# First weights and tokens in parts, the dense block's last h ahead of the next weights, the last expert h turned inside a down product

## The chip, the cores and the metric

One core of a Trainium2 chip runs the whole kernel. The metric is the device time of one execution in microseconds (us); a lower time is better.

## The reference, cut to what matters

Two layers over 256 tokens of width 1024, all float32. Each layer has a mixer and a feed-forward part, each followed by a LayerNorm of the scaled residual.

```python
for i in range(2):
    mix = hybrid_mixer(x, ...)           # proj = x @ w_in (1024 x 2560), split in b, c, h, u, v
    x = layer_norm(ALPHA * x + mix, ...) # gated short convolution | spatial gating of gelu(v); @ w_out
    if i % 2 == 0: ffn = (silu(x @ wg) * (x @ wu)) @ wd                  # dense, width 2816
    else:          ffn = sum over 8 experts, two chosen for each token   # width 3584 each
    x = layer_norm(ALPHA * x + ffn, ...)
```

## The kernel before, in words

**Tiling.** The 256 tokens are two tiles of 128. Weights come as 397 pieces of 1 MB (128 partitions x 2048 elements), numbered in the order of use. SyncE (SP) loads piece p into slot p % 6 of `raw` (`load`, L255) and waits, from piece 6 on, until piece p - 6 has been split. ScalarE (ACT) rounds a piece to `w_hi` (`split_hi`, L395), VectorE (DVE) writes the rest to `w_lo` (`split_lo`, L633), and TensorE (PE) makes each product as three matmuls: high by high, low by high, high by low (`product`, L1017). `w_hi` and `w_lo` have four places, so piece p waits until piece p - 4 has been used. The activations are split in the same way: `t_hi`/`t_lo` hold the turned tokens (xT), `a_hi`/`a_lo` the mixer output, the dense h or the gathered tokens of an expert, and `hT_hi`/`hT_lo` the turned h of an expert step.

**Order.** Every engine has its own list, written by hand; nothing is planned at run time.

**Start.** SP issues both token tiles (one DMA each), pieces 0 and 1 (the v columns of `w_in`), the two rows `v_g` and `v_b`, pieces 2 and 3, `w_s`, pieces 4 and 5, `b_s`, and so on (L267 to L292). PE turns both token tiles (`transpose_x(0, n)`, L1103), ACT and DVE split the turned tokens and then pieces 0 to 3 (L419, L721), and PE makes v for tile 0 and then tile 1, from piece 0 and then piece 1 (`tile_columns`, L1036; 24 matmuls of 256 columns for each of the four blocks). Then come two pieces with 48 such matmuls each (`two_blocks`, L1051), and then the transposes of `chan_rows` and `ws_raw`, for which GpSimd (POOL) must have masked `w_s` (L345).

**End of the dense block.** Groups of 256 hidden columns, j = 0 to 10. In group 10, ACT rounds piece 47 (the first of layer 1), waits for the gate and up products, takes the silu (L486), rounds piece 48 (L487) and then rounds h (L494). DVE multiplies (L826), splits piece 48 (L827) and then writes the rest of h (L830). PE ends with `last_rows` (L1085): for token tile 0 the down products of groups 9 and 10, then the same for tile 1. Before the last half of tile 1 it turns token tile 0, which DVE's `layer_norm` (L667) must have normalised.

**End of the experts.** 56 steps (8 experts x 7). In step i PE makes the gate product, turns the h of step i - 1 (`transpose_h`, L1242), makes the up product and then `down(i - 1)` (L1282), in two halves of 12 matmuls of 512 columns. After step 55 nothing is left but to turn its h, wait for ACT (L523) and DVE (L892) and make `down(55)`. Then the result is split, scattered to the tokens, added and normalised.

**Placement.** Tensors lie in SBUF in the order of their declaration (L82 to L122). `hT_hi`, `hT_lo`, `ys_hi`, `ys_lo`, `pickT` and the mixer's `work`, `v_rows`, `bs_rows` and `wsT` stand behind `chan`, `wr`, `small`, `eps_rms`, `neg_half` and `most_i`.

## Time and profile before

| | us |
|---|---|
| median of 3 runs | 1420.73 |
| lowest, highest | 1418.74, 1420.90 |
| the profiled execution | 1418.72 |
| its span in the trace | 1417.0 |
| PE busy | 1382.3 (98%) |
| DVE busy | 1120.4 (79%) |
| ACT busy | 905.2 (64%) |

The page of the profile has the busy time of each engine, the span in 40 slices, the DMA queues, the chain of work that ended last and the costliest groups of instructions. L12 is line 12 of the kernel. A wait is put down to what came last; idle time of an engine counts only where the end hangs on it. The granted clock is the share of PE's full clock (2.4 GHz); 0.50 is 1.2 GHz. The end of a matmul is modelled, so its pace is better read from the starts of matmuls that follow each other.

### The profile page before, as it was taken

Reading aid. Unit: us, or ns where it says so; the run is one execution under the profiler, and the core shown is the slowest. Engines: PE = TensorE matmul, PEld = TensorE weight load, DVE = VectorE, ACT = ScalarE, POOL = GpSimd, SP = SyncE. Lnnn points to the kernel's source line nnn. Section 1 sums busy time; section 2 is a strip of 40 time slices with the busy share of each in tenths; the row PEclk is TensorE's granted clock in tenths of the full one; section 3 lists DMA queues with packets and bytes.
Section 4 is the critical chain, followed back from the end, with each engine's and each line's share of the span. In section 5 each row is a group of like instructions: output and inputs, shape, how many; then the busy total and the mean of one; then the engine's idle time right before and its main releaser. Section 6 shows DMA issues by size and latency. Waiting matters only on the chain.

```text
span 1417.0 us, 17126 instructions
## 1 busy us (share of the span) xinstructions
PE 1382.3 (98%) x7250; PEld 1176.6 (83%) x7250; DVE 1120.4 (79%) x799; ACT 905.2 (64%) x657; POOL 21.5 (2%) x37
## 2 busy tenths in 40 slices
PE   7999999999999999999999999999999999999995
PEld 7979999989778888888888888888888888888883
DVE  6676454477779889879888988888898899889885
ACT  5374333444767777777677777777777676777771
POOL 1000000010000000000000000000000000000001
PEclk9999999999999999999999999999999999999998
DMA  9846655546459999999999999999999999999980
GB/s 324 307 143 220 194 181 180 191 137 215 141 176 391 367 353 365 348 338 365 360 349 348 357 361 337 363 364 344 348 359 354 349 364 364 342 353 353 365 321 31
DMA packets 202420, 425.89 MB, mean 301 GB/s; under 512 B 7740, under 2 KB 51812, under 8 KB 202340
## 3 DMA queue, kind: packets, MB, share of 16 engines
q1 hardware_dynamic: 201248, 421.06, 83.7%
q0 software_dynamic: 1024, 3.67, 0.8%
q8 instruction: 59, 0.97, 0.3%
q14 instruction: 21, 0.17, 0.0%
q10 hardware_dynamic: 68, 0.02, 0.0%
HBM read 423.68 MB, written 1.05 MB: 300 GB/s over the span
## 4 chain that ended last, share of the span: by engine, by line
PE 75%; DVE 2%; ACT 1%; issue 0%; DVEq 0%; ACTq 0%
PE turn L1020 15%; PE turn L1022 15%; PE turn L1021 15%; PE accp L1020 8%; PE accp L1022 8%; PE accp L1021 8%; PE accp L1245 2%; PE accp L1232 2%; PE accp L1272 1%; DVE w_lo L631 1%; ACT w_hi L400 0%; PE accp L1043 0%; PE accp L1048 0%; PE accp L1044 0%; PE turn L1272 0%; PE turn L1232 0%
## 5 line engine op out<-in xcount | busy, mean ns | idle before, releaser
L631 DVE TENSOR_TENSOR w_lo<-raw,w_hi 128x2048 fp32r<-128x2048 f32 x397 | 908.4, 2292 | 211.3 <-ACT w_hi L400 207.7
L400 ACT CAST w_hi<-raw 128x2048 fp32r<-128x2048 f32 x397 | 759.1, 1914 | 259.0 <-PE turn L1022 151.6
L1020 PE MATMUL turn<-w_hi,a_hi 128*128 128x512 f32 x888 | 352.8, 397 | 0.4 <-DVE w_lo L631 0.4
L1022 PE MATMUL turn<-w_hi,a_lo 128*128 128x512 f32 x888 | 347.4, 391 | 0.0
L1021 PE MATMUL turn<-w_lo,a_hi 128*128 128x512 f32 x888 | 346.1, 390 | 0.0
L1022 PEld LDWEIGHTS turn<-w_hi,a_lo 128*128 128x128 f32 x888 | 166.7, 188 | 36.6
L1021 PEld LDWEIGHTS turn<-w_lo,a_hi 128*128 128x128 f32 x888 | 167.0, 188 | 33.7
L1020 PEld LDWEIGHTS turn<-w_hi,a_hi 128*128 128x128 f32 x888 | 166.8, 188 | 33.7 <-DVE w_lo L631 0.8
L1020 PE MATMUL accp<-w_hi,hT_hi 128*128 128x512 f32 x448 | 178.5, 398 | 1.4 <-DVE hT_lo L631 1.4
L1022 PE MATMUL accp<-w_hi,hT_lo 128*128 128x512 f32 x448 | 176.9, 395 | 0.0
L1021 PE MATMUL accp<-w_lo,hT_hi 128*128 128x512 f32 x448 | 176.8, 395 | 0.0
L1020 PE MATMUL turn<-t_hi,w_hi 128*128 128x256 f32 x576 | 163.3, 283 | 0.0
L1022 PE MATMUL turn<-t_hi,w_lo 128*128 128x256 f32 x576 | 163.0, 283 | 0.0
L1021 PE MATMUL turn<-t_lo,w_hi 128*128 128x256 f32 x576 | 163.0, 283 | 0.0
L1021 PEld LDWEIGHTS turn<-t_lo,w_hi 128*128 128x128 f32 x576 | 110.5, 192 | 0.4
L1020 PEld LDWEIGHTS turn<-t_hi,w_hi 128*128 128x128 f32 x576 | 110.5, 192 | 0.3
L1022 PEld LDWEIGHTS turn<-t_hi,w_lo 128*128 128x128 f32 x576 | 110.5, 192 | 0.0
L1020 PEld LDWEIGHTS accp<-w_hi,hT_hi 128*128 128x128 f32 x448 | 84.4, 188 | 20.3 <-DVE hT_lo L631 1.6
L1022 PEld LDWEIGHTS accp<-w_hi,hT_lo 128*128 128x128 f32 x448 | 84.3, 188 | 20.0
L1021 PEld LDWEIGHTS accp<-w_lo,hT_hi 128*128 128x128 f32 x448 | 84.5, 189 | 18.8
L1020 PE MATMUL accp<-w_hi,a_hi 128*128 128x512 f32 x152 | 61.5, 405 | 3.5 <-DVE a_lo L631 3.5
L519 ACT ACTIVATE y_work<-turn 128x512 f32<-128x512 f32 x56 | 33.6, 599 | 46.0 <-PE turn L1022 40.6
(175 smaller groups left out, 958.1 us busy)
## 6 DMA issues: line engine op xcount, KB each, us to landing
raw<-in_we_gate SPq DMA_DIRECT2D x112, 1024.0 KB, 6.9
raw<-in_we_up SPq DMA_DIRECT2D x112, 1024.0 KB, 7.1
raw<-in_we_down SPq DMA_DIRECT2D x112, 1024.0 KB, 6.8
raw<-in_w_in SPq DMA_DIRECT2D x20, 1024.0 KB, 6.6
raw<-in_w_gate SPq DMA_DIRECT2D x11, 1024.0 KB, 5.3
raw<-in_w_up SPq DMA_DIRECT2D x11, 1024.0 KB, 5.3
raw<-in_w_down SPq DMA_DIRECT2D x11, 1024.0 KB, 5.0
raw<-in_w_out SPq DMA_DIRECT2D x8, 1024.0 KB, 7.6
```

The lines of the kernel that those rows point to most:

```text
L400: nc.scalar.copy(w_hi[:, p % PARTS, :], raw[:, p % RING, :]).then_inc(hi_done, 1)
L519: nc.scalar.activation(silu_e[:, i % 2, :], turn[:, 2 * (i % 2), :], ACT.Silu).then_inc(e_silu, 1)
L631: return nc.vector.tensor_tensor(out, whole, hi.bitcast(f32), ALU.subtract)
L1020: nc.tensor.matmul(to, lh, rh, start=start, stop=False, **group)
L1021: nc.tensor.matmul(to, lh, rl, start=False, stop=False, **group)
L1022: return nc.tensor.matmul(to, ll, rh, start=False, stop=stop, **group)
L1232: last = nc.tensor.matmul(to[:, k - k0, :], part[:, n, k * P:(k + 1) * P], pick[:, n, :], start=(n == 0), stop=(n == NT - 1))
L1245: last = nc.tensor.transpose(accp[:, 2, b * P:(b + 1) * P], h[:, b * P:(b + 1) * P], ident[:])
L1272: last = nc.tensor.matmul(to, pickT[:, n * P:(n + 1) * P], part[:, cols], start=(i == 0), stop=(i == 1))
```

## The change

- **Placement.** `chan` is made 64 elements wide in place of 40, `eps_rms` and `neg_half` move into unused columns of `small`, and `most_i` is made 16 elements wide. Tensors take whole steps of 32 bytes, so `wr`, `slot_iota`, `rank` and `small` move up by 96 bytes, and everything declared behind `most_i` by 96 - 64 + 32 = 64 bytes.
- **Start.** SP issues the columns of token tile 0 in two DMAs, piece 0 in four, token tile 1 in two and piece 1 in two. `v_g`, `v_b` move behind pieces 2 and 3, `w_s` behind pieces 4 and 5, `b_s` behind 6 and 7. PE makes six products of `ident` with itself ahead of the turning of tile 0 and four behind it. ACT and DVE split piece 0 in four parts and piece 1 in two. PE makes the v blocks in the order piece 0 tile 0, piece 0 tile 1, piece 1 tile 0, piece 1 tile 1, part by part, and turns tile 1 ahead of the last part of piece 0's first block. `split_done` and `hi_done` count from piece 2 on.
- **Gelu of tile 0.** ACT waits for the last matmul of tile 0's v instead of the next block's, in both layers.
- **End of the dense block.** In group 10 ACT takes the silu once the gate piece is used, and rounds h ahead of piece 48; DVE waits for the up piece ahead of the multiplication, and writes the rest of h ahead of piece 48.
- **End of the experts.** PE turns the h of step 55 between the halves of `down(54)`. ACT and DVE split it in halves of 256 columns, the second when `down(54)` has ended, and the second half of `down(55)` waits for it.

The diff, cut to its core (`first_hi` and `first_lo` of before are also renamed to `slots_hi` and `slots_lo`):

```diff
+    FIRST = ((0, 0, 2), (0, 2, 4), (0, 4, 6), (0, 6, 8), (1, 0, 4), (1, 4, 8))
     def dense_gate(j):
...
-        chan = sb("chan", [P, N_CHAN])
+        chan = sb("chan", [P, 64])
         wr = sb("wr", [P, KD, E])
...
         small = sb("small", [P, 208])
-        eps_rms = sb("eps_rms", [P, 1])
-        neg_half = sb("neg_half", [P, 1])
-        most_i = sb("most_i", [1, 1], i32)
+        most_i = sb("most_i", [1, 16], i32)
         with ExitStack() as mixers:
...
         rstd = small[:, 20:24]
+        eps_rms = small[:, 24:25]
+        neg_half = small[:, 25:26]
         logits = small[:, 32:48].rearrange("p (n e) -> p n e", n=NT)
...
-        x_loaded = [sem(f"x_loaded{n}") for n in range(NT)]
+        x_loaded = [[sem(f"x_loaded{n}{half}") for half in range(2)] for n in range(NT)]
+        first_filled = [sem(f"first_filled{c}") for c in range(len(FIRST))]
+        first_hi, first_split, v0_done = sem("first_hi"), sem("first_split"), sem("v0_done")
         ws_loaded, chan_loaded, vrows_loaded, bs_loaded, ln_loaded, wr_loaded = (
...
             return p + 1
+        def split_of(p):
+            return (first_split, (4, 6)[p]) if p < 2 else (split_done, p - 1)
+        def fills(p):
+            return p // RING + (1 if p % RING > 1 else 0)
         def transposed(build, n, half=1):
...
                 if p >= RING:
-                    sp.wait_ge(split_done, upto(p - RING))
+                    sp.wait_ge(*split_of(p - RING))
                 dst = raw[:, p % RING, :].rearrange("p (k f) -> p k f", k=src.shape[1])
...
                     for half in range(2):
-                        load(at + 2 * i + half, columns(w_in[l], c0 + half * HALF))
+                        if l or i:
+                            load(at + 2 * i + half, columns(w_in[l], c0 + half * HALF))
                     between(i)
...
             def small_inputs(i):
+                if i == 2:
+                    sp.dma_start(ws_raw, w_s.rearrange("l h t s -> t (l h) s")).then_inc(ws_loaded, 16)
                 if i == 1:
-                    sp.dma_start(ws_raw, w_s.rearrange("l h t s -> t (l h) s")).then_inc(ws_loaded, 16)
-                if i == 0:
                     for j, a in enumerate((v_g, v_b)):
                         sp.dma_start(v_rows[:, j, :], a[0].partition_broadcast(P)).then_inc(vrows_loaded, 16)
-                if i == 2:
+                if i == 3:
                     sp.dma_start(bs_rows[:], b_s.partition_broadcast(P)).then_inc(bs_loaded, 16)
...
                     sp.dma_start(wr[:], w_router[0].rearrange("(k p) e -> p k e", p=P)).then_inc(wr_loaded, 16)
-            for n in range(NT):
-                sp.dma_start(x[:, n, :], x_in[0, n * P:(n + 1) * P, :]).then_inc(x_loaded[n], 16)
+            def load_x(n):
+                for half in range(2):
+                    cols = slice(half * BANK, (half + 1) * BANK)
+                    sp.dma_start(x[:, n, cols], x_in[0, n * P:(n + 1) * P, cols]).then_inc(x_loaded[n][half], 16)
+            def load_first(p):
+                src = columns(w_in[0], 3 * CW + GW + p * HALF)
+                dst = raw[:, p, :].rearrange("p (k f) -> p k f", k=KD)
+                for c, (piece, k0, k1) in enumerate(FIRST):
+                    if piece == p:
+                        sp.dma_start(dst[:, k0:k1, :], src[:, k0:k1, :]).then_inc(first_filled[c], 16)
+            load_x(0)
+            load_first(0)
+            load_x(1)
+            load_first(1)
             mixer(0, 0, small_inputs)
...
-                act.wait_ge(slot_filled[p % RING], 16 * (p // RING + 1))
+                act.wait_ge(slot_filled[p % RING], 16 * fills(p))
                 if p >= PARTS:
...
+            def first_parts(p):
+                for c, (piece, k0, k1) in enumerate(FIRST):
+                    if piece == p:
+                        act.wait_ge(first_filled[c], 16)
+                        part = slice(k0 * HALF, k1 * HALF)
+                        nc.scalar.copy(w_hi[:, p, part], raw[:, p, part]).then_inc(first_hi, 1)
             for n in range(NT):
                 round_tile(0, n)
-            splits(0, 3)
+                first_parts(n)
+            splits(2, 3)
             for l in range(DEPTH):
...
                 for n in range(NT):
-                    used(at + n)
+                    if n:
+                        used(at + 1)
+                    else:
+                        act.wait_ge(v0_done, l + 1)
                     nc.scalar.activation(v[:, n, :], accp[:, n, :], ACT.Gelu).then_inc(v_gelu, 1)
...
                             split_hi(p)
-                        used(dense_up(j))
+                        used(dense_up(j) if j < GROUPS - 1 else dense_gate(j))
                         gate = accp[:, 0:2, 0:HALF] if j == 0 else turn_half[:, 4 * (j % 2):4 * (j % 2) + 2, :]
                         nc.scalar.activation(silu_buf[:, j % 2], gate, ACT.Silu).then_inc(silu_ready, 1)
-                        split_hi(p + 1)
+                        if j < GROUPS - 1:
+                            split_hi(p + 1)
                         if j == 0:
...
                             nc.scalar.copy(h_hi[:, j % 2], h_buf[:, j % 2]).then_inc(h_hi_ready, 1)
-                        if j < GROUPS - 1:
-                            split_hi(p + 2)
+                        split_hi(p + 2 if j < GROUPS - 1 else p + 1)
                     round_tile(2, 0)
...
+            def round_last_h():
+                act.wait_ge(e_hT, N_STEPS)
+                for half in range(2):
+                    if half:
+                        used(step_down(N_STEPS - 2) + 1)
+                        act.wait_ge(e_hT_lo, N_STEPS)
+                    cols = slice(half * HALF, (half + 1) * HALF)
+                    nc.scalar.copy(hT_hi[:, cols], accp[:, 2, cols]).then_inc(e_hT_hi, 1)
             def round_ys(e):
...
             split_hi(MOE_AT + MOE_PIECES - 1)
-            round_h(N_STEPS - 1)
+            round_last_h()
             round_ys(E - 1)
...
-                dve.wait_ge(hi_done, upto(p))
+                dve.wait_ge(hi_done, p - 1)
                 rest_of(w_lo[:, p % PARTS, :], raw[:, p % RING, :], w_hi[:, p % PARTS, :]).then_inc(split_done, 1)
...
             last.then_inc(mean_conv_ready, 1)
-            for n in range(NT):
-                rest_of_tile(0, n)
-            splits(0, 3)
+            def first_part(c):
+                p, k0, k1 = FIRST[c]
+                dve.wait_ge(first_hi, c + 1)
+                part = slice(k0 * HALF, k1 * HALF)
+                rest_of(w_lo[:, p, part], raw[:, p, part], w_hi[:, p, part]).then_inc(first_split, 1)
+            for half in range(2):
+                rest_of_xT(0, 0, half, turn[:, half, :].rearrange("p (k t) -> p k t", t=P))
+                first_part(half)
+            first_part(2)
+            first_part(3)
+            rest_of_tile(0, 1)
+            first_part(4)
+            first_part(5)
+            splits(2, 3)
             for l in range(DEPTH):
...
                         dve.wait_ge(silu_ready, j + 1)
+                        used(dense_up(j))
                         nc.vector.tensor_tensor(h_buf[:, j % 2], up, silu_buf[:, j % 2], ALU.mult).then_inc(h_whole, 1)
-                        split_lo(p + 1)
+                        if j < GROUPS - 1:
+                            split_lo(p + 1)
                         dve.wait_ge(h_hi_ready, j + 1)
...
                         rest_of(h_lo[:, j % 2], whole, h_hi[:, j % 2]).then_inc(h_ready, 1)
-                        if j < GROUPS - 1:
-                            split_lo(p + 2)
+                        split_lo(p + 2 if j < GROUPS - 1 else p + 1)
                     layer_norm(1, MIX1_AT - 1)
...
                 rest_of(hT_lo[:], accp[:, 2, :], hT_hi[:]).then_inc(e_hT_lo, 1)
+            def rest_of_last_h():
+                for half in range(2):
+                    dve.wait_ge(e_hT_hi, N_STEPS + half)
+                    cols = slice(half * HALF, (half + 1) * HALF)
+                    rest_of(hT_lo[:, cols], accp[:, 2, cols], hT_hi[:, cols]).then_inc(e_hT_lo, 1)
             def rest_of_ys(e):
...
             split_lo(MOE_AT + MOE_PIECES - 1)
-            rest_of_h(N_STEPS - 1)
+            rest_of_last_h()
             def finish_experts():
...
-                if build == 0:
-                    pe.wait_ge(x_loaded[n], 16)
                 for half in range(2):
-                    if build:
+                    if build == 0:
+                        pe.wait_ge(x_loaded[n][half], 16)
+                    else:
                         pe.wait_ge(ln_norm, transposed(build - 1, n, half))
...
                         pe.wait_ge(xT_ready, transposed(build, n, 2 * k // KD))
+                    last = nc.tensor.matmul(to, xT_lo[:, k, tile], wh[:, k, :], start=False, stop=(k == KD - 1))
+                return last
+            def first_columns(p, n, to, before_last=None):
+                tile = slice(n * P, (n + 1) * P)
+                wh, wl = [a[:, p, :].rearrange("p (k f) -> p k f", k=KD) for a in (w_hi, w_lo)]
+                for c, (piece, k0, k1) in enumerate(FIRST):
+                    if piece != p:
+                        continue
+                    if k1 == KD and before_last is not None:
+                        before_last()
+                    pe.wait_ge(first_hi, c + 1)
+                    for k in range(k0, k1):
+                        if k in (0, KD // 2):
+                            pe.wait_ge(xT_hi_ready, transposed(0, n, 2 * k // KD))
+                        nc.tensor.matmul(to, xT_hi[:, k, tile], wh[:, k, :], start=(k == 0), stop=False)
+                    pe.wait_ge(first_split, c + 1)
+                    for k in range(k0, k1):
+                        nc.tensor.matmul(to, xT_hi[:, k, tile], wl[:, k, :], start=False, stop=False)
+                for k in range(KD):
+                    if k in (0, KD // 2):
+                        pe.wait_ge(xT_ready, transposed(0, n, 2 * k // KD))
                     last = nc.tensor.matmul(to, xT_lo[:, k, tile], wh[:, k, :], start=False, stop=(k == KD - 1))
...
                             last.then_inc(piece_used, 1)
+            def warm(count):
+                for _ in range(count):
+                    nc.tensor.matmul(turn[:, 3, 0:P], ident[:], ident[:], start=True, stop=True)
             pe.wait_ge(ident_ready, 1)
-            for n in range(NT):
-                transpose_x(0, n)
+            warm(6)
+            transpose_x(0, 0)
+            warm(4)
+            for half in range(2):
+                for n in range(NT):
+                    last = first_columns(half, n, accp[:, n, half * HALF:(half + 1) * HALF],
+                                         (lambda: transpose_x(0, 1)) if half == 0 and n == 0 else None)
+                    if n:
+                        last.then_inc(piece_used, 1)
+                    elif half:
+                        last.then_inc(v0_done, 1)
             for l in range(DEPTH):
                 at = l * MIX1_AT
-                for n in range(NT):
-                    if l and n:
+                for n in range(NT if l else 0):
+                    if n:
                         transpose_x(2, 1)
                     for half in range(2):
-                        last = tile_columns(at + half, 2 * l, n, accp[:, n, half * HALF:(half + 1) * HALF])
+                        last = tile_columns(at + half, 2, n, accp[:, n, half * HALF:(half + 1) * HALF])
                         if n:
                             last.then_inc(piece_used, 1)
+                        elif half:
+                            last.then_inc(v0_done, 1)
                 for i in range(2):
...
                 for half in range(2):
+                    if half and i == N_STEPS - 2:
+                        pe.wait_ge(e_h, N_STEPS)
+                        transpose_h(h_e[:, (N_STEPS - 1) % 2, :]).then_inc(e_hT, 1)
+                    if half and i == N_STEPS - 1:
+                        pe.wait_ge(e_hT_lo, N_STEPS + 1)
                     half_down(half, split(step_down(i) + half), s == 0 and half == 0,
...
-                if i:
+                if 0 < i < N_STEPS:
                     pe.wait_ge(e_h, i)
```

## Rows read from the trace of the kernel before

**Rows 1.** The page: its span, and the busy time of each engine.
```profile
span 1417.0 us, 17126 instructions
...
PE 1382.3 (98%) x7250; PEld 1176.6 (83%) x7250; DVE 1120.4 (79%) x799; ACT 905.2 (64%) x657; POOL 21.5 (2%) x37
```

**Rows 2.** PE's waits: waiting line, awaited line, us in all, times, longest.
```profile
PE accp L1043 <- DVE w_lo L631: 5.2, 1, 5.2
...
PE accp L1020 <- DVE a_lo L631: 3.5, 3, 2.7
...
PE accp L1020 <- DVE hT_lo L631: 1.4, 1, 1.4
```

**Rows 3.** Timeline of the start: start, us, engine, line, operation, idle before and releaser.
```profile
1.24 0.29 POOL L329 TENSOR_SCALAR_AFFINE_SELECT ident<-ident 128x128 f32<-128x128 f32 x1 [0.24 <-POOL ident L327]
...
4.57 3.36 PE L1033 MATMUL turn<-ident,x 128*128 128x128 f32 x16 [4.57 <-DMA x<-in_x]
...
8.85 1.90 ACT L400 CAST w_hi<-raw 128x2048 fp32r<-128x2048 f32 x1 [0.30 <-DMA raw<-in_w_in]
...
13.13 0.58 PE L1043 MATMUL accp<-w_hi,t_hi 128*128 128x256 f32 x1 [5.20 <-DVE w_lo L631]
...
17.23 1.91 ACT L400 CAST w_hi<-raw 128x2048 fp32r<-128x2048 f32 x1 [3.52 <-DMA raw<-in_w_in]
...
18.12 0.28 PE L1043 MATMUL accp<-w_hi,t_hi 128*128 128x256 f32 x1
...
22.09 1.09 POOL L345 TENSOR_SCALAR_AFFINE_SELECT y_work<-y_work 128x1024 f32<-128x1024 f32 x1 [19.28 <-DMA y_work<-in_w_s]
...
26.75 0.28 PE L1020 MATMUL turn<-t_hi,w_hi 128*128 128x256 f32 x1
```

**Rows 4.** Windows of the start: busy us (count) by engine, granted clock, DMA share, GB/s.
```profile
5.00:10.00 5.00, 2.92 (x16) 2.69 (x14) 2.67 (x4) 3.47 (x5) 0.00 (x0) 1.00 1.08 358
10.00:15.00 5.00, 1.87 (x8) 1.88 (x9) 3.55 (x2) 2.65 (x2) 0.00 (x0) 0.59 1.06 307
```

**Rows 5.** Timeline of the end of the dense block.
```profile
281.92 0.60 ACT L486 ACTIVATE y_work<-turn 128x512 f32<-128x512 f32 x1 [3.81 <-PE turn L1022]
...
282.55 0.69 DVE L826 TENSOR_TENSOR y_work<-turn,y_work 128x512 f32<-128x512 f32 x1 [2.11 <-ACT y_work L486]
...
284.21 0.62 ACT L494 CAST a_hi<-y_work 128x512 fp32r<-128x512 f32 x1
...
284.24 0.39 PE L1022 MATMUL accp<-w_hi,a_lo 128*128 128x512 f32 x1
...
287.30 0.74 PE L1020 MATMUL accp<-w_hi,a_hi 128*128 128x512 f32 x1 [2.67 <-DVE a_lo L631]
...
290.28 0.69 DVE L677 SCALAR_TENSOR_TENSOR x<-x,accp 128x512 f32<-128x512 f32 x1 [3.03 <-issue]
...
295.15 1.42 DVE L692 SCALAR_TENSOR_TENSOR x<-x,small,ln_rows 128x512 f32<-128x512 f32 x2
...
295.96 1.32 PE L1033 MATMUL turn<-ident,x 128*128 128x128 f32 x8
```

**Rows 6.** A window behind that wait, with the columns of rows 4.
```profile
288.00:289.00 1.00, 1.00 (x4) 0.81 (x3) 0.00 (x0) 0.00 (x0) 0.00 (x0) 0.50 0.89 250
```

**Rows 7.** Timeline of the end of the experts.
```profile
1386.46 2.28 DVE L631 TENSOR_TENSOR w_lo<-raw,w_hi 128x2048 fp32r<-128x2048 f32 x1
...
1389.77 0.60 PE L1245 MATMUL accp<-ident,y_work 128*128 128x128 f32 x4
...
1391.77 0.51 PE L1020 MATMUL accp<-w_hi,hT_hi 128*128 128x512 f32 x1 [1.40 <-DVE hT_lo L631]
```

**Rows 8.** The page's groups: count, busy us, mean ns of one, idle before.
```profile
L631 DVE TENSOR_TENSOR w_lo<-raw,w_hi 128x2048 fp32r<-128x2048 f32 x397 | 908.4, 2292 | 211.3 <-ACT w_hi L400 207.7
...
L1021 PE MATMUL turn<-w_lo,a_hi 128*128 128x512 f32 x888 | 346.1, 390 | 0.0
...
L1021 PE MATMUL accp<-w_lo,hT_hi 128*128 128x512 f32 x448 | 176.8, 395 | 0.0
```

32 lines of the change are left out of this document (16 added, 16 removed).

## Prediction

> **What bounds the kernel now.** I read the page first: PE is busy for 1382.3 of 1417.0 us, so only what lets PE work without a gap, or work less, can move the end [rows 1]. Then I read PE's own waits, to see where the other 35 us are [rows 2]: one wait of 5.2 us for the split of piece 0, behind a start in which PE has nothing but two token tiles; one of 2.7 us (the longest of three on that line) for the last dense h; one of 1.4 us for the last expert h. The change has one part for each. The timelines around these three places give the durations [rows 3, 5, 7], the windows give the clock and the rate of the transfers [rows 4, 6], and the page's groups show what else the change touches [rows 8]. Between the three places PE is the engine that others wait for, so what is won at one place shifts all that follows (the transfers behind the first six pieces wait for freed slots, L257).
>
> **The start, PE's side.** Before, the v blocks begin at 13.13 and the fourth ends at 26.75. The first block's 24 matmuls take 4.99 us (0.208 each), the next 72 take 8.63 us (0.120 each) [rows 3]: PE came out of a pause of 5.2 us, the granted clock is 0.59 on average between 10 and 15 us [rows 4], and the pace says it went from 1.2 to 2.4 GHz just ahead of 18.12.
>
> **The start, transfers.** Two tiles and piece 0 are 2.10 MB and have landed at 8.85 [rows 3]; the rate is 358 GB/s [rows 4]. So a transfer that ends after c MB lands at 8.85 - (2.10 - c) / 0.358. In the new order: tile 0 at 3.7 and 4.4, the quarters of piece 0 at 5.2, 5.9, 6.6 and 7.4, tile 1 at 8.85, the halves of piece 1 at 10.3 and 11.8, piece 2 at 14.7 (it was 17.23 [rows 3]), piece 3 at 17.6.
>
> **The start, the chain.** `ident` is ready at 1.53. A transpose took 0.21 us (3.36 / 16) [rows 3]; the trace has no product of `ident` with itself, so each costs 0.21 as the transpose does, or 0.42 if a product in full float32 takes two such passes. I take 0.42: the six end at 4.1, with no loss against tile 0 at 3.7 to 4.4 beyond 0.4 us. Tile 0 is turned by 5.8. ACT takes 0.62 us for 512 columns [rows 5]: the two halves of tile 0 end at 5.8 and 6.65, the quarters of piece 0 at 7.3, 7.9, 8.5 and 9.15, each behind its landing. DVE takes 0.69 us for 512 [rows 5], in its order: rest of quarter 0 until 8.05, second half of tile 0 until 8.75, quarters 1, 2 and 3 until 9.45, 10.15 and 10.85. So PE, which follows the quarters, is limited by DVE. It ends quarter 2 at 10.45, turns tile 1 (8 x 0.12) until 11.4, makes quarter 3 (4 x 0.12) and the eight matmuls with the tokens' low part by 12.9. Three more blocks of 24 x 0.12 = 2.88 end at 21.5. Before it was 26.75: **5.2 us** earlier. The four products behind tile 0 run from 5.8 to 7.5 at most, while PE has nothing to do until 7.3, so they cost nothing.
>
> **The start, what is late next.** Piece 1: ACT needs 1.05 us for 1024 columns (between 0.62 for 512 and 1.90 for 2048), DVE 1.22 in the same way from 0.69 and 2.29 [rows 3, 5, 8]; behind tile 1 that gives 14.5 and 15.7 for its halves, and PE asks at 15.8 and 16.8. Piece 2 lands at 14.7, is split at 18.9 and wanted at 21.5. The moved small tensors: `v_g` and `v_b` land with piece 3, near 20, ahead of the first gelu. `w_s` was there at 22.09 with 6.29 MB issued, 1.5 us later than the line above gives; now 8.39 MB precede its end, so 28 to 29.5, the mask takes 1.1 [rows 3], and PE asks at 21.5 + 96 x 0.12 = 33.0. Cover of 2.4 us; if it is gone, each further microsecond costs one. SP issues ten DMAs for four, ahead of data that moves for 9 us; nothing waits for SP there.
>
> **The clock in the start.** Both ends: if the low clock lasted until 17.7 as it did before, quarter 3 and tile 1 would end at 14.7 instead of 12.9, some 14 matmuls more would run at 0.208, and the fourth block would end at 24.6: a gain of 2.1. If the products cost 0.21 and the clock is up early, the chain moves by 0.8: a gain of 6.0. I take 5.2, because PE is now busy from 1.6 to 7.5 almost without a gap, longer than the 4.6 us of work after which the clock rose before, and no idle stretch behind it is over 1.4 us. The Trainium skill, TensorE: Matmul & The Clock Gate (What's actually happening), says that the low clock is the default and activity lifts it; by that rule the added products do what the rows lead me to take.
>
> **The end of the dense block.** PE's 12 matmuls of tile 0 with group 9 start at 281.72 (284.24 - 11 x 0.229) and the next could start at 284.47; it started at 287.30 [rows 5], and the microsecond after 288 shows 4 matmuls at granted clock 0.50 [rows 6], 0.43 each against 0.23, for about 3.4 us: 2.8 us of waiting and 1.6 us of low clock. Now DVE multiplies from 281.95 to 282.65, ACT rounds h until 283.3 (0.62), DVE ends the rest at 284.05 (0.69): 0.4 us ahead of PE's need, so both are gone for PE. But piece 48 now comes behind: ACT until 285.2, DVE until 287.5 (2.29 [rows 8]), and only then can the LayerNorm begin, which could have begun at 286.1. It began at 290.28 and reached its last step at 295.15, and PE turned the tile at 295.96 [rows 5]. With its start at 287.5 and 0.2 us of waiting gone, PE turns it at 293.0: **2.9 us** earlier. PE has work only until 284.47 + 30 x 0.229 = 291.3, so a new wait of 1.7 us stands there. Bounds: 4.4 if the LayerNorm were no limit, 1.2 if the new wait costs the clock again (1.7 us, half of 3.4). The added wait of DVE for the up piece holds nothing in groups 0 to 9, where the silu waited for it already.
>
> **The end of the experts.** `down(54)` starts at 1384.2 (24 x 0.232 ahead of 1389.77) and its half at 1387.0; the h of step 55 is ready at 1386.5, just ahead of DVE's piece at 1386.46 to 1388.74 [rows 7]. The four transposes cost 0.48 there (4 x 0.12), as they did behind. ACT and DVE have the first half of h at 1389.2, and `down(55)` starts at 1384.2 + 24 x 0.232 + 0.48 = 1390.25 instead of 1391.77; the second half of h comes near 1391.2 and is wanted at 1393.0. **1.5 us** earlier; bounds 1.0 and 1.6. The gelu of tile 0 in layer 1 may start earlier; no wait of PE hangs on it: nothing.
>
> **The realigned tensors.** Not one row of ACT or DVE hangs on them. What moves and matters is `hT_hi` and `hT_lo`: their 1344 matmuls take 395 ns each where those with `a_hi` and `a_lo` take 390 [rows 8]. That difference may come from where they lie; a move by 64 bytes may then take it away (-6.7 us, 1344 x 0.005), leave it, or raise it by as much. I take nothing: the rows do not show which address is good. The Trainium skill, SBUF — State Buffer (Two separate sides, the note on cachelines), knows lines of 16 bytes only; both places begin on one, so by it nothing changes either.
>
> **Sum.** 5.2 + 2.9 + 1.5 = 9.6 us. The profiled execution took 1418.72, its span 1417.0, with 1.7 us around it; it gives 1409.1. The median is 2.0 us above that execution, so the median comes to **1411.1 us**.
>
> **Rivals.**
> (a) The clock stays low through the first blocks, because PE works in short bursts between 7.5 and 12.9: the start gives 2.1. 1414.2 us. For it: the 0.50 behind a gap of 2.7 us [rows 5, 6]; against it: the gaps here are half as long. 12%.
> (b) The new wait of 1.7 us at the dense end brings the low clock back: 1412.8 us. 8%.
> (c) The change doesn't do what it says at the start, since transfers in small parts are slower or land in no order: at 307 GB/s in place of 358 [rows 4], the 3.15 MB up to piece 1 and the 2.10 up to tile 1 come 1.0 to 1.5 us later, and PE, held by tile 1 at 10.45, loses up to as much with each of them, and piece 2 loses its cover: a gain of 1 to 3 in place of 5.2. 1414.5 us. The Trainium skill, SBUF — State Buffer (The DMA setup-cost knee), speaks against this part of the change: it wants the largest single transfer; by its 224 GB/s for 256 KB, an estimate of mine puts tile 1 at 12.3 in place of 8.85, some 2 us too late for PE. 8%.
> (d) The move of `hT` takes the 5 ns away: 1404.4 us. 8%.
> (e) Slower than before: the move of `hT` makes each of its 1344 matmuls slower. From 7.1 ns on (9.6 / 1344) it eats the whole gain; at twice the difference of the rows, 10 ns, it gives 1424.5 us. 4%; below 7 ns, near 1418, another 2%.
>
> The forecast itself has 58%.
>
> **How the numbers follow.** The forecast holds 1409 to 1412.5 by its terms; (a), (b) and (c) lie up to 1416. The range 1407.5 to 1416.5 takes these in, with 1.5 us for the scatter of the median, and leaves (d) and (e) out: 14% and the tails. 0.2% of 1420.73 is 2.8 us, about what a measurement of this kernel can tell from no change. Faster than that, below 1417.9: 94%; within it: 3%; slower: 3%.
>
> **What would show it.** In the changed kernel the first `two_blocks` matmul starts near 21.5 and its clock is 1.00 from about 9 us on; a start near 24.5 with 0.50 before is (a); PE waiting for a DMA is (c). No wait for the dense h, the transposes of the next tile near 288 (293.0 less 5.2), a wait of 1.7 us for the normalised x ahead of them, clock 1.00. No wait for `hT_lo` at the end. The mean of `accp<-w_lo,hT_hi` at 395 ns; 390 is (d), over 400 is (e). A `w_s` mask later than 33 us would make the prediction wrong at a place where I see cover.

## The result, and the profile after

The changed kernel takes **1406.3 us** (median of 13 executions, 1403.84 to 1416.54; before on the same chips 1420.73, 1418.19 to 1421.84). The ratio is 0.9904, 95% interval 0.9889 to 0.9918: faster, by 14.4 us where 9.6 were forecast. The sign, and the 2 us between a median and its profiled execution, came out as written; the time lies 1.2 us below the low end of the range of 1407.5 to 1416.5. One of the 13 executions took 1416.54 at a granted clock of 0.986; nothing here explains it.

The page of the changed kernel answers [rows 1]: the profiled execution took 1404.18, its span is 14.8 us shorter, and PE's busy time is 5.6 us shorter although 20 records were added. Work itself has become quicker, not only waits.

```profile
span 1402.2 us, 17198 instructions
PE 1376.7 (98%) x7270; PEld 1176.3 (84%) x7270; DVE 1119.4 (80%) x804; ACT 905.6 (65%) x662; POOL 21.4 (2%) x37
```

PE's waits in the changed kernel (waiting line, awaited line, us in all, times, longest), against [rows 2]. The waits of 5.2, 2.7 and 1.4 us are gone; what stands in their place is the wait for the normalised `x`, whose longest was 1.3 and is 1.5.

```profile
PE turn L1104 <- DVE x L742: 3.3, 4, 1.5
...
PE turn L1091 <- DVE w_lo L681: 1.1, 2, 0.7
PE accp L1091 <- DVE a_lo L681: 0.8, 2, 0.4
```

The timeline of the start (start, us, engine, line, operation, idle before and releaser), against [rows 3]:

```profile
1.58 2.93 PE L1199 MATMUL turn<-ident 128*128 128x128 f32 x12 [1.58 <-POOL ident L357]
...
4.30 1.91 PE L1104 MATMUL turn<-ident,x 128*128 128x128 f32 x8
...
6.01 1.12 PE L1199 MATMUL turn<-ident 128*128 128x128 f32 x8
...
7.41 0.51 PE L1135 MATMUL accp<-w_hi,t_hi 128*128 128x256 f32 x2 [0.28 <-ACT w_hi L453]
...
10.28 1.03 PE L1104 MATMUL turn<-ident,x 128*128 128x128 f32 x8
...
13.41 1.05 ACT L453 CAST w_hi<-raw 128x1024 fp32r<-128x1024 f32 x1 [0.43 <-DMA raw<-in_w_in]
...
14.49 1.23 DVE L681 TENSOR_TENSOR w_lo<-raw,w_hi 128x1024 fp32r<-128x1024 f32 x1 [0.25 <-ACT w_hi L453]
...
16.42 1.91 ACT L428 CAST w_hi<-raw 128x2048 fp32r<-128x2048 f32 x1 [1.96 <-DMA raw<-in_w_in]
...
16.91 0.64 PE L1138 MATMUL accp<-w_lo,t_hi 128*128 128x256 f32 x4
...
21.23 0.28 PE L1091 MATMUL turn<-t_hi,w_hi 128*128 128x256 f32 x1
```

The end of the dense block, against [rows 5]: h is split ahead of piece 48, PE never waits for it, and the LayerNorm (L727) starts right behind DVE's piece.

```profile
278.33 0.62 ACT L535 CAST a_hi<-y_work 128x512 fp32r<-128x512 f32 x1 [4.10 <-DVE y_work L890]
...
278.99 0.69 DVE L681 TENSOR_TENSOR a_lo<-y_work,a_hi 128x512 fp32r<-128x512 f32 x1 [0.69 <-ACT a_hi L535]
280.80 2.29 DVE L681 TENSOR_TENSOR w_lo<-raw,w_hi 128x2048 fp32r<-128x2048 f32 x1 [1.12 <-ACT w_hi L428]
283.00 0.68 DVE L727 SCALAR_TENSOR_TENSOR x<-x,accp 128x512 f32<-128x512 f32 x1
...
287.70 1.41 DVE L742 SCALAR_TENSOR_TENSOR x<-x,small,ln_rows 128x512 f32<-128x512 f32 x2 [0.22 <-DVE x L735]
288.51 1.32 PE L1104 MATMUL turn<-ident,x 128*128 128x128 f32 x8 [1.46 <-DVE x L742]
```

Two windows around that wait, with the columns of [rows 4]: the granted clock (third figure from the end) stays at 1.00, where [rows 6] has 0.50.

```profile
284.00:286.00 2.00, 2.00 (x11) 1.65 (x10) 1.90 (x4) 0.00 (x0) 0.00 (x0) 1.00 0.78 259
286.00:288.00 2.00, 1.05 (x5) 0.55 (x3) 1.77 (x4) 0.00 (x0) 1.00 (x1) 1.00 0.76 266
```

The end of the experts, against [rows 7]: the last h is turned 12 matmuls earlier, and no wait stands between it and the last product.

```profile
1374.05 0.60 PE L1355 MATMUL accp<-ident,y_work 128*128 128x128 f32 x4
...
1375.79 0.42 DVE L681 TENSOR_TENSOR hT_lo<-accp,hT_hi 128x256 fp32r<-128x256 f32 x1
...
1377.86 0.42 DVE L681 TENSOR_TENSOR hT_lo<-accp,hT_hi 128x256 fp32r<-128x256 f32 x1 [1.65 <-ACT hT_hi L573]
```

And the page's groups, against [rows 8]. The products with `a_hi` stand still at 390 ns; those with `hT_hi` went from 395 to 392.

```profile
L1092 PE MATMUL turn<-w_lo,a_hi 128*128 128x512 f32 x888 | 346.0, 390 | 0.0
...
L1092 PE MATMUL accp<-w_lo,hT_hi 128*128 128x512 f32 x448 | 175.7, 392 | 0.0
```

**Where the 14.75 us of the span went.** I cut both spans at the same seven matmuls, read from the timelines. For before these are the first of `two_blocks` at 26.75 [rows 3] (26.76 unrounded), the turning of token tile 0 at 101.49 (end of layer 0's mixer) and at 295.96 (end of the dense block, [rows 5]), that of tile 1 in the router stage at 391.74, and the first and last product with `hT`; three of the rows, of before:

```profile
101.49 1.21 PE L1033 MATMUL turn<-ident,x 128*128 128x128 f32 x7 [0.29 <-DVE x L692]
...
426.99 0.40 PE L1020 MATMUL accp<-w_hi,hT_hi 128*128 128x512 f32 x1
...
1397.22 0.40 PE L1022 MATMUL accp<-w_hi,hT_lo 128*128 128x512 f32 x1
```

and of the changed kernel:

```profile
97.07 0.66 PE L1104 MATMUL turn<-ident,x 128*128 128x128 f32 x4 [0.27 <-DVE x L742]
...
419.51 0.39 PE L1091 MATMUL accp<-w_hi,hT_hi 128*128 128x512 f32 x1
...
1382.52 0.39 PE L1093 MATMUL accp<-w_hi,hT_lo 128*128 128x512 f32 x1
```

| stretch | before | changed | difference | forecast |
|---|---|---|---|---|
| start, to the first `two_blocks` | 26.76 | 21.23 | -5.53 | -5.2 |
| mixer of layer 0 | 74.73 | 75.84 | **+1.11** | 0 |
| dense block, to the turned tile | 194.47 | 191.44 | -3.03 | -2.9 |
| mixer of layer 1, to the tile of the router stage | 95.78 | 95.75 | -0.03 | 0 |
| router stage, to the first product with `hT` | 35.25 | 35.25 | 0.00 | 0 |
| experts, first to last product with `hT` | 970.23 | 963.01 | **-7.22** | -1.5 |
| what follows | 19.76 | 19.71 | -0.05 | 0 |

The fourth stretch ends at 391.74 and 384.26. The start and the dense block are met within 0.4 us. Two stretches are not: the mixer of layer 0 gives back 1.1, and the experts gain 5.7 more than was forecast for the last h.

### The profile page after: what moved, and what is told of

Its sections match the earlier page's. It is cut to its first block, busy times and chain, and to the rows that moved or that the text cites. A ratio compares the mean times of both kernels' runs of the same rounds, so it can differ in the third digit from the quotient of the medians.

```text
span 1402.2 us, 17198 instructions
## 1 busy us (share of the span) xinstructions
PE 1376.7 (98%) x7270; PEld 1176.3 (84%) x7270; DVE 1119.4 (80%) x804; ACT 905.6 (65%) x662; POOL 21.4 (2%) x37
## 4 chain that ended last, share of the span: by engine, by line
PE 90%; DVE 4%; ACT 3%; SPq 1%; DMA 1%; issue 1%; POOL 0%; DVEq 0%; ACTq 0%
PE turn L1091 19%; PE turn L1093 19%; PE turn L1092 19%; PE accp L1091 9%; PE accp L1092 9%; PE accp L1093 9%; PE accp L1355 2%; PE accp L1342 2%; DVE w_lo L681 1%; PE accp L1382 1%; DMA y_work<-in_w_s 1%; ACT w_hi L428 1%; PE accp L1114 1%; SPq L272 1%; PE accp L1119 1%
## 5 line engine op out<-in xcount | busy, mean ns | idle before, releaser
L681 DVE TENSOR_TENSOR w_lo<-raw,w_hi 128x2048 fp32r<-128x2048 f32 (+1 forms) x401 | 907.9, 2269 | 204.3 <-ACT w_hi L428 200.1
L1091 PEld LDWEIGHTS accp<-w_hi,hT_hi 128*128 128x128 f32 x448 | 84.2, 188 | 17.7
```

What stands on the lines that cost most here:

```text
L681: return nc.vector.tensor_tensor(out, whole, hi.bitcast(f32), ALU.subtract)
L1091: nc.tensor.matmul(to, lh, rh, start=start, stop=False, **group)
```

## The experiments

Times of kernels are compared with before on the same chip. One execution of each kernel has a trace. Over these 14 traces three stretches repeat within 0.06 us where nothing in them was changed, and tell more than the medians: the dense block in its new order (191.41 to 191.45), the mixer of layer 1 (95.74 to 95.80) and the experts (within 0.02). The others differ between executions: the start with all ten products of `ident` takes 20.62 to 21.37 us, the mixer of layer 0 with the changed kernel's order 75.02 to 76.16, the router stage 35.2 to 38.7, and what follows the experts 18.7 to 19.8.

**1. Before, with `hT` moved by 64 bytes.** Is it the address of `hT` that makes the experts quicker? The edit, on the kernel before:

```diff
+        hT_pad = sb("hT_pad", [P, 16])
         hT_hi = sb("hT_hi", [P, COL], f32r)
```

> The kernel before with one edit: 64 unused bytes are declared ahead of hT_hi, so that hT_hi, hT_lo, ys_hi, ys_lo and pickT alone lie 64 bytes higher; chan, small, most_i and the mixer's tensors stay. Theory P (the place of hT sets the pace of the down products): the down products, 24 matmuls, go from 5.36 to 5.27 us (starts of first to last), accp<-w_lo,hT_hi from 395 to 392 ns, and the time falls by 56 x 0.096 = 5.4 us, to 1415.3. Rival Q (the pace fell because the small tensors or the work tensors moved, or because of the order of the work): 1420.7, 395 ns stays.

Measured: 1412.17 us against 1418.73, ratio 0.9956 (0.9941 to 0.9970). The experts' stretch takes 964.67 instead of 970.23, 5.57 us less. One padding tensor does well over a third of what the whole change does (5.57 of 14.75). It also moves `ys_hi`, `ys_lo` and `pickT`, and no run moves these alone; but 4.6 of the 5.57 us lie between the starts of neighbouring products with `hT`, so these are the main part. Another 0.97 us of the profiled execution lies in what follows the experts, which differs by as much between executions without this edit.

**2. The changed kernel with the small tensors placed as before.** The other side of the same question:

```diff
-        chan = sb("chan", [P, 64])
+        chan = sb("chan", [P, N_CHAN])
...
-        most_i = sb("most_i", [1, 16], i32)
+        eps_rms = sb("eps_rms", [P, 1])[:, :]
+        neg_half = sb("neg_half", [P, 1])[:, :]
+        most_i = sb("most_i", [1, 1], i32)
```

> The changed kernel with the placement of before (chan of 40 columns, eps_rms, neg_half and most_i as tensors of their own): everything else of the change stays. Theory P and rival Q with small tensors as the cause: 1406.3 + 5.4 = 1411.7 us, accp<-w_lo,hT_hi back at 395 ns. Rival Q with the order as the cause: 1406.3 us, 392 ns. The sum of my forecast without the placement was 1411.1.

Measured: 1412.05, ratio 0.9949 (0.9932 to 0.9965). The stretch takes 968.56; with the new placement it takes 963.01, 5.55 us less. The same amount from both kernels, and 968.56 against before's 970.23 leaves 1.67 us for the last h.

**3 and 4. `hT` moved further.** The changed kernel with 64 and with 192 bytes ahead of `hT_hi` (the same edit as in 1). In the compiled kernels `w_hi`, `w_lo` and the `a` and `t` tensors start at an address whose remainder by 256 is 128. For `hT_hi` it is 0 before, 64 in the changed kernel, 128 in the first of these runs and 0 again in the second.

> The changed kernel with 64 more unused bytes ahead of hT_hi, which puts hT at 128 bytes above a multiple of 512, as w_hi, w_lo, a_hi and a_lo lie. Theory P1 (the stationary operand is read without loss only where it lies as a_hi does): the steady pace goes from 229 to the 227 ns of the products with a_hi, 1344 x 0.0023 = 3 us less, 1403.2. Theory P2 (64 bytes off the old place is what counts): slower again than 1406.3, towards 1411.7. Rival Q: 1406.3.

> The changed kernel with 192 more unused bytes ahead of hT_hi: 256 above a multiple of 512. Theory P1: the pace of before or between, 229 to 233 ns, 1406 to 1411.7 us. If only the remainder by 256 counts, this is the place of before: 233 ns and 1411.7. Rival Q: 1406.3.

Measured: 1402.44, ratio 0.9879 (0.9863 to 0.9896), with the stretch at 960.10; and 1411.79, ratio 0.9947 (0.9930 to 0.9963), with the stretch at 968.56. So the pattern repeats after 256 bytes: the address 256 higher gives the stretch of the old place (run 2).

**5 and 6. Which rule?** Best at remainder 128: because that is a good place by itself, because it is the middle, or because the weights lie there too? In the first run `hT` is at 192 (128 bytes ahead of it). In the second the weights, the tokens and `hT` all move by 128 bytes against run 3, so all have remainder 0:

```diff
+        front_pad = sb("front_pad", [P, 32])
         raw = sb("raw", [P, RING, PIECE])
...
+        hT_pad = sb("hT_pad", [P, 16])
         hT_hi = sb("hT_hi", [P, COL], f32r)
```

> The changed kernel with 128 more unused bytes ahead of hT_hi: 192 above a multiple of 256, where before has 0, the change 64 and the best run so far 128. The 24 matmuls of a down product took 5.36, 5.27 and 5.21 us there. Theory M (what counts is the distance from 128, the remainder at which the weights w_hi and w_lo lie): 5.27 us and the time of the change, 1406.3. Rival N (the further up within 256 bytes the better): 5.21 us or less, 1403.

> 128 unused bytes ahead of raw and 64 ahead of hT_hi: every large tensor (raw, w_hi, w_lo, t, a) and hT now lie on a multiple of 256. Theory R (the stationary operand is best where its remainder by 256 equals that of the moving operand): all products at the best pace, 227 ns, time as with hT at 128: about 1403. Rival A (the place of the stationary operand alone counts, 0 is bad): the down products at 233 ns as before (+8.7 us against 1403) and the 2688 matmuls with a_hi and a_lo in the expert steps too, up to 6.5 ns each: another 17 us, about 1429.

Measured: 1409.94, ratio 0.9934 (0.9915 to 0.9953), stretch 968.28; and 1401.93, ratio 0.9870 (0.9854 to 0.9887), stretch 960.11. The second settles it: remainder 0 is as good as 128 if the weights have it too, and as bad as it was before if they haven't. What counts is how `hT` stands to the tensors ahead of it. All of these moved together, so the run doesn't single out one; the products with `hT` read only `w_hi` and `w_lo` of them, and I take it to be these. The page's group of these products, of before, of run 1, of run 3, of run 5 and of run 6, one fence each:

```profile
L1021 PE MATMUL accp<-w_lo,hT_hi 128*128 128x512 f32 x448 | 176.8, 395 | 0.0
```
```profile
L1022 PE MATMUL accp<-w_lo,hT_hi 128*128 128x512 f32 x448 | 175.7, 392 | 0.0
```
```profile
L1093 PE MATMUL accp<-w_lo,hT_hi 128*128 128x512 f32 x448 | 174.3, 389 | 0.0
```
```profile
L1093 PE MATMUL accp<-w_lo,hT_hi 128*128 128x512 f32 x448 | 177.1, 395 | 0.0
```
```profile
L1094 PE MATMUL accp<-w_lo,hT_hi 128*128 128x512 f32 x448 | 174.3, 389 | 0.0
```

| `hT` less weights, by 256 | runs | experts' stretch | against the best, per product |
|---|---|---|---|
| 0 | 3, 6, 11, 12 | 960.09 to 960.11 | 0 |
| -64 | changed, 7, 8, 9 | 963.01 | 2.2 ns |
| -128 | 2, 4 | 968.56 | 6.3 ns |
| +64 | 5 | 968.28 | 6.1 ns |

The last column is the difference divided by 1344. A matmul with 512 columns of the weights and 128 x 128 of `hT` as the operand that is loaded starts every 227 ns at best, as most of those with `a_hi` and `a_lo` do in all these kernels; at +64 the distances between starts alternate between 231 and 236 ns, and at -128 they run through a longer pattern from 228 to 241 ns.

**7. GpSimd's mask of `w_s` behind the first rstd.** What costs the mixer of layer 0 1.1 us? In the changed kernel GpSimd waits for `w_s` at the head of its list, and the power for v of token tile 0 (L378) is queued behind it; DVE (L797) waits for that power, and the split of the next piece is queued behind DVE's. The rows of the changed kernel:

```profile
28.92 1.09 POOL L373 TENSOR_SCALAR_AFFINE_SELECT y_work<-y_work 128x1024 f32<-128x1024 f32 x1 [26.11 <-DMA y_work<-in_w_s]
...
29.98 0.57 POOL L378 TENSOR_TENSOR small<-small 128x1 f32<-128x1 f32 x1
30.59 0.55 DVE L797 TENSOR_SCALAR work<-work,small 128x512 f32<-128x512 f32 x1 [5.95 <-POOL small L378]
...
34.85 0.39 PE L1091 MATMUL turn<-t_hi,w_hi 128*128 128x256 f32 x1 [0.74 <-DVE w_lo L681]
```

```diff
-            pool.wait_ge(ws_loaded, 16)
-            nc.gpsimd.affine_select(out=ws_raw, ...).then_inc(ws_masked, 1)
...
                 for n in range(NT):
                     power(v_var, v_rstd, n, NT * l + n + 1)
+                    if l == 0 and n == 0:
+                        pool.wait_ge(ws_loaded, 16)
+                        nc.gpsimd.affine_select(out=ws_raw, ...).then_inc(ws_masked, 1)
```

> The changed kernel with one move: GpSimd waits for w_s and masks it behind the power of v's tile 0 instead of ahead of it. Theory: in the changed kernel that power stood behind the wait for w_s (until 28.9 us), DVE waited 5.95 us for it, piece 4 was split late and PE waited 0.7 us; of the 5.5 us won by the first four blocks 1.1 was gone at the end of the mixer. So the turning of the tile behind the mixer comes at 96.0 in place of 97.07 and the time is 1405.2. Rival (the transfers behind it are late themselves): nothing, 1406.3.

Measured: 1404.46, ratio 0.9898 (0.9881 to 0.9914). In its timeline DVE's wait is 0.70 instead of 5.95, and PE has no wait between 26 and 41 us:

```profile
25.46 0.58 POOL L375 TENSOR_TENSOR small<-small 128x1 f32<-128x1 f32 x1 [22.65 <-DVE small L716]
26.08 0.55 DVE L798 TENSOR_SCALAR work<-work,small 128x512 f32<-128x512 f32 x1 [0.70 <-POOL small L375]
...
29.25 1.99 POOL L391 TENSOR_SCALAR_AFFINE_SELECT y_work<-y_work 128x1024 f32<-128x1024 f32 x1 [3.21 <-DMA y_work<-in_w_s]
```

The mixer's stretch takes 74.74, before's 74.73 (and 74.72 and 74.73 in runs 11 and 12, with the same order): the 1.1 us are this wait and nothing else. How much it costs changes with each execution, since the end of the mixer hangs on the landing of `w_s`: in all nine traces with the changed kernel's order, token tile 0 is turned 68.14 to 68.17 us after the mask starts, and that start lies anywhere from 28.17 (run 6) to 29.23 (run 9). Run 6:

```profile
28.17 1.09 POOL L375 TENSOR_SCALAR_AFFINE_SELECT y_work<-y_work 128x1024 f32<-128x1024 f32 x1 [25.37 <-DMA y_work<-in_w_s]
...
96.32 1.32 PE L1106 MATMUL turn<-ident,x 128*128 128x128 f32 x8 [0.25 <-DVE x L744]
```

 The median alone would not have said so (its ratio is 0.9898 where the changed kernel's is 0.9904, well within both intervals).

**8. No products of `ident`.** What are the ten products at the start worth? Both calls of `warm` are taken out of the changed kernel.

> The changed kernel without the ten products of ident with itself. Theory (they brought the high clock to the first blocks): tile 0 is turned 0.5 us earlier, the clock of the first blocks is 0.50 for 4 to 8 us, the first two_blocks matmul comes at 23.0 to 24.6 in place of 21.23, the time is 1408.1 to 1409.7. Rival (the transposes and the quarters alone bring the clock): 21.2 or a little earlier, 1406.3.

Measured: 1405.68, ratio 0.9900 (0.9884 to 0.9917). By the pace of PE's records the clock rises at 12.7 us instead of 6.1, and the first `two_blocks` matmul stands at 22.30 instead of 21.23: 1.1 us. But at the end of layer 0's mixer nothing of this is left. The tile is turned 0.25 us later than in the changed kernel, and the mask starts 0.24 later: that is the landing of `w_s`, not the products. With `w_s` landing this late the ten products were worth nothing to the whole. Where it lands earliest (run 6, the tile turned at 96.32) they can be worth up to 0.7 us, an estimate: 22.30 + 74.73 = 97.03 without them. Whether they give all of their 1.1 us once the mask is out of the way (run 7) no run shows. Here PE turns tile 0 as soon as it lands:

```profile
3.64 1.96 PE L1104 MATMUL turn<-ident,x 128*128 128x128 f32 x8 [3.64 <-DMA x<-in_x]
...
29.16 1.09 POOL L373 TENSOR_SCALAR_AFFINE_SELECT y_work<-y_work 128x1024 f32<-128x1024 f32 x1 [26.35 <-DMA y_work<-in_w_s]
...
97.32 1.32 PE L1104 MATMUL turn<-ident,x 128*128 128x128 f32 x8 [0.27 <-DVE x L742]
```

**9. The end of the dense block undone.** The changed kernel with the order of before in group 10 on ACT, and the same on DVE:

```diff
-                        used(dense_up(j) if j < GROUPS - 1 else dense_gate(j))
+                        used(dense_up(j))
...
-                        if j < GROUPS - 1:
-                            split_hi(p + 1)
+                        split_hi(p + 1)
...
-                        split_hi(p + 2 if j < GROUPS - 1 else p + 1)
+                        if j < GROUPS - 1:
+                            split_hi(p + 2)
```

> The changed kernel, only the end of the dense block put back to the order of before: in group 10 the silu waits for the up product, and piece 48 is split ahead of h on both engines. My theory (the last dense h held PE, then the LayerNorm; worth 3.0 us, the difference of the marks 288.51 and 295.96 less the 4.4 that were ahead at the start): PE waits 2.7 us again for the rest of h, the clock falls to 0.50 for some 3 us behind it, the LayerNorm begins 2.8 to 3 us later, and token tile 0 is turned near 291.5 instead of 288.5; no wait for the normalised x ahead of it. Time of a profiled execution near 1407.2, median 3 us above the changed kernel's, near 1409.3. Rival (the new wait of 1.5 us takes most of it back, so the part is worth 1.5 or less): near 1407.5. Rival (the low clock behind the wait comes only by chance, not with the wait): the tile near 290, 1407.8.

Measured: 1408.13, ratio 0.9916 (0.9900 to 0.9933). The wait and the low clock are back, as in the two other traces with the old order (before and run 1), and the dense block's stretch takes 194.69, 3.25 us more than in the changed kernel; before and run 1, with 194.47 and 194.32, take 3.0 and 2.9 more:

```profile
283.23 0.50 PE L1091 MATMUL accp<-w_hi,a_hi 128*128 128x512 f32 x1 [2.67 <-DVE a_lo L681]
...
286.00:287.00 1.00, 1.00 (x4) 0.76 (x3) 0.89 (x2) 0.00 (x0) 0.00 (x0) 0.50 1.02 357
```

The profiled execution is 4.9 us longer (1409.10 against 1404.18): 3.25 of it here, 2.2 in the router stage (below), 0.3 in the mixer of layer 0, less 0.9 behind the experts. The median moved by 1.8 only, with four executions in place of 13; the others have no trace, so why it moved by less than this stretch is open.

**10. The end of the experts undone.** The changed kernel with `round_h`, `rest_of_h`, `down` and the turning of h as before for step 55.

```diff
-            round_last_h()
+            round_h(N_STEPS - 1)
...
-                    if half and i == N_STEPS - 2:
-                        pe.wait_ge(e_h, N_STEPS)
-                        transpose_h(h_e[:, (N_STEPS - 1) % 2, :]).then_inc(e_hT, 1)
-                    if half and i == N_STEPS - 1:
-                        pe.wait_ge(e_hT_lo, N_STEPS + 1)
...
-                if 0 < i < N_STEPS:
+                if i:
```

> The changed kernel, only the end of the experts put back: the h of step 55 is turned behind the down product of step 54, and split whole. My theory (worth 1.5 us): a wait of 1.4 us for the rest of h in front of the last down product, last h turned 24 matmuls behind the start of the product of step 54, span 1.5 us longer, 1403.7; median near 1407.8. The pace of the 1344 products stays at 392 ns by the page's measure, since no address moves. Rival (the turning within the product cost PE as much as it saved, so the part is worth 0.3 or less, and all of the last 7 us came from the addresses): span 1402.5, median near 1406.5.

Measured: 1408.48, ratio 0.9919 (0.9903 to 0.9936). The wait is back, and the experts' stretch takes 964.66, 1.65 us more; run 1, with the same order and the same distance, has 964.67. The span of this execution is 4.5 us longer than the changed kernel's, more than I expected: the rest is the router stage (38.29 instead of 35.25).

```profile
1381.65 0.50 PE L1091 MATMUL accp<-w_hi,hT_hi 128*128 128x512 f32 x1 [1.40 <-DVE hT_lo L681]
```

**11 and 12. All together, and the clock of the router stage.** The router stage takes 35.2 us in before, the changed kernel and runs 1, 2 and 7, but 37.5 in runs 3, 4, 5, 9 and 12, and 38.3 to 38.7 in runs 6, 8 and 10, with the clock at 0.50 for 7 to 10 us of it; run 11 lies between. Two windows of the same stretch, of the changed kernel and of run 12:

```profile
387.00:389.00 2.00, 2.00 (x12) 1.74 (x13) 1.86 (x6) 1.95 (x2) 0.00 (x0) 1.00 1.01 369
```
```profile
387.00:389.00 2.00, 2.00 (x7) 1.71 (x8) 1.12 (x7) 0.55 (x1) 0.00 (x0) 0.50 0.99 268
```

Run 11 is the changed kernel with `hT` at remainder 128 (run 3), the later mask (run 7) and five more filling products in front of the second tile's turning, where PE waits 1.34 us; run 12 has the first two alone.

```diff
-                    keep_clock(4, 0)
+                    keep_clock(9, 0)
                     transpose_x(3, 1)
```

> The changed kernel with three things the runs pointed to: the turned h moved on to 128 by 256 (as in the run with that move, 1402.4), GpSimd's mask of w_s placed behind the first rstd of tile 0 (as in the run with that order, worth 1.1 to 1.7 us by the marks at the mixer's end), and nine instead of four filling products ahead of the turning of the second token tile in the router stage (five more of 0.227 us in a wait of 1.34 us). Theory: the first two add, so that the span is near 1399.5 where the clock is up throughout; the filling products keep the clock at 1.00 between 383 and 394 us in every execution, so that the scatter between executions shrinks to under 1 us and the median stands within 1 us of the profiled time: 1400. Rival (the pause is not what lets the clock fall there; what goes before it is): some executions still show 0.50 there, median 1401 to 1402, spread of 3 us as before. Rival (the mask's gain is only the earlier clock of that execution): 1401 even with the clock up.

> As the run with all three, but with four filling products as in the changed kernel. Tells the clock of the router stage apart from the rest. Theory: executions in two groups some 2.3 us apart (1399.5 to 1400.5 with the clock up, 1402 to 1403 with it at 0.50 for 7 to 10 us between 383 and 394 us), median between 1400 and 1402, up to 2 us above the run with nine. Rival (filling products change nothing): the same median and spread as that run.

Measured: run 11 takes **1399.26** (1398.71 to 1399.73), ratio 0.9854 (0.9838 to 0.9871), and run 12 1400.41 (1399.71 to 1402.22), ratio 0.9865 (0.9846 to 0.9883). The two gains add: the mixer's stretch is 74.72 and 74.73, the experts' 960.10 and 960.09. The filling products take the wait in front of the tile from 1.34 to 0.16 us, but they don't keep the clock:

```profile
383.04 1.32 PE L1106 MATMUL turn<-ident,x 128*128 128x128 f32 x8 [0.16 <-DVE x L744]
...
388.00:389.00 1.00, 1.00 (x4) 0.81 (x3) 0.83 (x6) 0.00 (x0) 0.00 (x0) 0.50 0.81 213
```

So the clock falls without that wait too, as the rival said, and the cause is open. In this execution the clock is at 0.50 for some 3 us, and the stage takes 35.91. The scatter is 1.0 instead of 2.5 us, but with four executions each and overlapping intervals I call the 1.15 us between 11 and 12 not shown. Run 11 beats the changed kernel by 7 us, by the medians and by the ratios (0.0050 of 1420 us).

## Why the prediction was right, and where it failed

Two steps of the prediction failed. The one that put the time below the range is the term for the realigned tensors, taken as nothing: it was worth 5.55 us. The other is the cover of 2.4 us for `w_s`: it cost 1.1 us. The three terms that were forecast came to 10.2 us where 9.6 stood.

**The start.** Right in amount (5.53 against 5.2) and by its own chain: the first v matmul at 7.41, tile 1 turned at 10.28 (10.45 forecast), `two_blocks` at 21.23 (21.5). A product of `ident` shows as two records: 12 records, six products, from 1.58 to the turning at 4.30, 0.43 us each once they run. Rival (a) did not come: the eight records behind tile 0 take 0.14 us each where the twelve ahead of it took 0.24, so the clock rose near 6.1 us, ahead of the 9 us I gave. The rise at 17.7 us that I argued from was not the only one in the trace of before: by the pace of its records (0.21, then 0.11 us) the clock had risen at 7.5, 2.9 us into the turning, and it fell at 10.9, in the pause of 5.2 us that the new start doesn't have. Run 8 has (a)'s low clock in part: it is up at 12.7, where (a) let it stay low until 17.7, and its start still gains 4.5 us. What the low clock until 17.7 would cost no run shows. Nor does a run undo the new start as a whole, so how the 5.5 us divide between smaller parts and new order is not shown.

**The transfers** were worse than I wrote, and it cost nothing. The second half of piece 1 was cast at 13.41 as soon as it landed, 1.6 us behind my line (11.8), and behind the 11.81 at which the whole of piece 1 landed before; piece 2 came at 16.42, not 14.7. That is rival (c)'s delay, 1.0 to 1.5 us there. Its price didn't come, because it ate idle time of ACT and only 0.25 us of DVE's: DVE had the rest of piece 1 at 15.72 (14.49 + 1.23) and PE asked at 16.91, a cover of 1.2 us where I had counted 1.1. The row of before:

```profile
11.81 1.90 ACT L400 CAST w_hi<-raw 128x2048 fp32r<-128x2048 f32 x1 [1.06 <-DMA raw<-in_w_in]
```

The Trainium skill, SBUF — State Buffer (The DMA setup-cost knee), gives 224 GB/s for 256 KB; here 2.88 MB in parts of 256 and 512 KB landed between 3.64 (run 8) and 13.41, 295 GB/s, so transfers that queue behind each other lost less than that figure for one transfer. Before, with parts of 0.5 and 1 MB, 2.62 MB landed between 4.57 and 11.81, 362 GB/s.

**What is late next** is the step that failed behind the start. I had `w_s` right (landed at 28.9, between 28 and 29.5) and its mask right, and asked only when PE wants the masked tensor. The order of GpSimd's list was not followed: the power for v stands behind the mask, and DVE's later split behind the power. 1.1 us lost (run 7), in a place where I wrote cover of 2.4. In the execution of run 8 it also hid what the ten products of `ident` win.

**The end of the dense block.** Right, 3.03 against 2.9: h's rest ended at 279.68, PE didn't wait, the LayerNorm began at 283.00 behind piece 48 and bounds the stretch, with a new wait of 1.46 (1.7 forecast) and no low clock, so rival (b) fell. Undone, it costs 3.25 (run 9).

**The last expert h.** Right: 1.65 (run 10) and 1.67 (run 2 against before), 1.5 forecast. The earlier gelu in layer 1 is worth nothing, as forecast: the stretch of its mixer is 95.75 against 95.78.

**The realigned tensors** are the term that failed. I named the mechanism, rival (d), and its bound of 6.7 us, and then took nothing and gave it 8%, "the rows do not show which address is good". Measured: 5.55 us (runs 1 and 2), 4.1 ns for each of the 1344 products. The old place was the worst of the four that the runs tried; the rows of before couldn't show that. They did show equal shapes 5 ns apart, which made an effect of place, for better or worse, more likely than the 14% of (d) and (e) together. That is hindsight: `a` and `hT` products also differ in what stands around them. The Trainium skill, SBUF — State Buffer (Two separate sides, the note on cachelines), knows lines of 16 bytes; by it these moves change nothing. The runs disagree: 64 bytes are worth 5.6 us (run 1).

**The sum**: -5.53 + 1.11 - 3.03 - 1.65 - 5.55 and -0.1 in the rest is -14.75, the difference of the spans. Without the two missed terms it would have been 10.3.

**The median** lies 2.1 us above the profiled execution (2.0 forecast; that was carried over from before, without a cause, so the match is luck). The likeliest reason is the router stage: 0.7 to 3.5 us longer where its clock falls, which it did in nine of the twelve profiled experiments and not in the two executions that the tables compare. The start, the mixer of layer 0 and what follows the experts differ by up to 1.1 us each and add to it. The mean granted clock of the executions agrees: 0.995 in the three at 1403.8 to 1404.2, 0.994 at 1405.3 to 1405.6, 0.993 in the six at 1406.3 to 1406.9. Only one of them has a trace, so the place was not seen and the reason is not shown.

## What to carry to other kernels

When a change moves a tensor that PE reads all the time, compare the group means of equal products in the profile first: 4 ns on each of 1344 matmuls was worth as much as the whole new start, and a padding tensor tests it. When a transfer is made later, follow the list of the engine that waits for it, not only the consumer of its data: what is queued behind the wait is delayed as well, and a part that wins time ahead of that wait, as the products of `ident` did, can lose it all there. And measure a part by its stretch between two fixed instructions, after checking that the stretch repeats where nothing was changed: executions of one kernel scattered by 3 us, more than most parts were worth.

## What the runs showed of the hardware

- The pace of the 128x128x512 matmuls with `hT` changed with how the address of `hT` (the operand that is loaded) stood to that of the weights (the one that streams), by 256 bytes: equal remainders gave 227 ns, 64 below 2.2 ns more on the mean, 128 apart 6.3 more, 64 above 6.1 more. The address of `hT` alone doesn't decide (run 6). That it is not symmetric is unexplained, and so is what in the chip the two share.
- The granted clock of the same stage differs between executions of one kernel: it rose between 4.5 (run 11) and 7.7 us in the start of the kernels with all ten products (by the pace of PE's records), and in the router stage it fell to 0.50 in nine of 14 traces, for 3 to 10 us, with PE in a stage of narrow matmuls and a wait of 1.34 us in it. With that wait down to 0.16 us it fell as well (run 11); the cause is open.
- Transfers of 256 and 512 KB in a queue landed at 295 GB/s, those of 0.5 and 1 MB at 362, and the same 3.15 MB were there 1.6 us later.
- Where GpSimd's power stood behind its wait for `w_s`, the end of layer 0's mixer followed the start of the mask by 68.14 to 68.17 us in nine traces.
